# Half of the last weight block stays on chip, and the gathers get six, seven and eleven slots in place of seven, nine and eleven

## The reference

```python
merged = sigmoid(g_nsa) * (o_nsa @ w_br_nsa) + sigmoid(g_dsa) * (o_dsa @ w_br_dsa)
x = x + g1 * (merged @ w_out)
h = rms_norm(x, norm2_g) * (1.0 + sc2) + sh2
q = (h @ peer_wq).reshape(T, 8, 2, 64)                  # the query
s_sub = einsum("thcd,hcnd->thcn", q, subkeys)           # product keys, top 16 -> eidx, gate
for chunk in two chunks of 128 tokens:
    ue, ve = u[ec], v[ec]                               # 128 experts per token, 8 KB each
    act = gelu(einsum("cd,chkd->chk", xc, ue))
    out = einsum("chk,chkd->cd", gc * act, ve)
```

## Time and profile before

| | us |
|---|---|
| median of 3 runs | 981.22 (981.1 to 983.23) |
| profiled execution, its own time | 977.82 |
| profiled execution, span from first to last instruction | 976.0 |
| busy in the span: PE / DVE / ACT / POOL | 800.7 / 645.1 / 409.1 / 283.5 |
| mean granted clock of TensorE | 0.957 of full |

### The profile page before, as it was taken

The page is one execution under the profiler, slowest core; times in us unless marked ns, Lnnn a source line. Parts: engine busy times, 40 slices in busy tenths (PEclk is TensorE's granted clock), DMA queues, the critical chain, the costliest instruction groups (busy, mean ns, idle before and its releaser), DMA issues.

```text
span 976.0 us, 9734 instructions
## 1 busy us (share of the span) xinstructions
PE 800.7 (82%) x2940; PEld 445.9 (46%) x2940; DVE 645.1 (66%) x1663; ACT 409.1 (42%) x1148; POOL 283.5 (29%) x260
## 2 busy tenths in 40 slices
PE   4899969999888989887787788697777778777775
PEld 3644557888873544444454354232322222222221
DVE  4521446996359897886766866867858667586644
ACT  4101132223246887633243634544544344343433
POOL 0000000000033544453343435354253442534420
PEclk8699979998999999999999999999899999999998
DMA  9982403768049999999999999999999999999993
GB/s 373 424 332 92 173 1 111 321 259 344 24 170 424 412 419 419 373 422 418 420 418 419 421 419 420 422 420 422 422 422 421 422 422 421 421 422 422 420 422 125
DMA packets 46899, 342.84 MB, mean 351 GB/s; under 512 B 5312, under 2 KB 6528, under 8 KB 10624
## 3 DMA queue, kind: packets, MB, share of 16 engines
q0 software_dynamic: 36864, 268.45, 66.5%
q1 hardware_dynamic: 9536, 73.31, 18.9%
q10 hardware_dynamic: 448, 0.46, 0.2%
HBM read 341.16 MB, written 1.05 MB: 351 GB/s over the span
## 4 chain that ended last, share of the span: by engine, by line
DMA 45%; PE 27%; DVE 14%; ACT 6%; issue 4%; POOL 2%; SPq 0%; DVEq 0%; POOLq 0%
DMA extra<-in_uv,arena 27%; DMA arena<-in_uv,arena 9%; PE banks L470 7%; DMA ring<-in_uv,arena 7%; PE banks L711 6%; PE banks L504 5%; DVE extra L1480 3%; DMA extra<-in_w_ada 3%; PE banks L664 1%; DVE arena L1480 1%; PE banks L653 1%; PE banks L683 1%; ACT L1002 1%; ACT extra L1012 1%; PE banks L587 1%
## 5 line engine op out<-in xcount | busy, mean ns | idle before, releaser
L711 PE MATMUL banks<-extra 128*128 128x512 f32 x500 | 243.5, 620 | 59.3 <-ACT extra L1012 59.2
L802 POOL DMA_INDIRECT extra<-in_uv,arena x136 | 152.2, 1119 | 459.4 <-DVE arena L1463 315.0
L1002 ACT ACTIVATE arena<-arena 128x1 f32<-128x1 f32 x256 | 51.7, 202 | 323.8 <-DVE arena L1480 323.3
L711 PE MATMUL banks<-arena,extra 128*128 128x512 f32 x296 | 149.1, 633 | 40.0 <-ACT extra L1012 40.0
L711 PEld LDWEIGHTS banks<-extra 128*128 128x128 f32 x500 | 88.7, 193 | 193.5 <-ACT extra L1012 113.9
L1480 DVE CUSTOM_DVE_ANT_0 extra<-extra 128x1024 f32<-128x1024 f32 x80 | 97.9, 1227 | 51.1 <-DMA extra<-in_uv,arena 49.9
L802 POOL DMA_INDIRECT arena<-in_uv,arena x80 | 86.2, 1078 | 129.4 <-PE banks L711 56.4
L711 PEld LDWEIGHTS banks<-arena,extra 128*128 128x128 f32 x296 | 52.9, 196 | 126.9 <-ACT extra L1012 83.7
L1012 ACT ACTIVATE extra<-tab,arena 128x128 f32<-128x128 f32 x235 | 94.3, 401 | 7.7
L1480 DVE CUSTOM_DVE_ANT_0 extra<-extra,arena 128x1024 f32<-128x1024 f32 x56 | 68.6, 1225 | 42.4 <-DMA extra<-in_uv,arena 41.7
L711 PE MATMUL banks<-ring,extra 128*128 128x512 f32 x144 | 73.6, 638 | 26.0 <-ACT extra L1012 26.0
(11 more groups left out here) (242 smaller groups left out, 1064.8 us busy)
## 6 DMA issues: line engine op xcount, KB each, us to landing
arena<-in_w_ada SPq DMA_DIRECT2D x8, 2048.0 KB, 12.1
arena<-in_w_late SPq DMA_DIRECT2D x24, 512.0 KB, 8.3
extra<-in_w_ada SPq DMA_DIRECT2D x4, 2048.0 KB, 10.3
arena<-in_w_in SPq DMA_DIRECT2D x3, 2048.0 KB, 27.4
extra<-in_w_gate SPq DMA_DIRECT2D x3, 2048.0 KB, 8.3
extra<-in_w_br SPq DMA_DIRECT2D x2, 2048.0 KB, 13.9
arena<-in_w_wq SPq DMA_DIRECT2D x2, 2048.0 KB, 18.6
extra<-in_uv,arena POOLq DMA_INDIRECT x136, 18.9
```

Source lines behind the costliest of these rows:

```text
L711: last = nc.tensor.matmul(acc[tt][:, half * 512:(half + 1) * 512], diag[i % DIAGS], uv_slot[SLOT[v]][:, D + half * 512:D + (half + 1) * 51 ...
L802: nc.gpsimd.indirect_dma_start(uv_slot[SLOT[g]], None, A["uv"], bass.IndirectOffsetOnAxis(ap=expert[:, g:g + 1], axis=0)).then_inc(uv_in[S ...
L1002: link(nc.scalar.activation(gel[:, v:v + 1], dots[:, v:v + 1], ACT.Gelu))
```

## The change

Four of the eight query pieces are no longer in the list; the second tile's query takes m 4 to 7 from the 2 MB block that the first tile used, which stays in arena[0:4D] until then. The three late buffers are now arena[4D:5D], arena[5D:6D] and ring[2D:3D]. The gathers have 6 slots up to value 53, 7 up to 123 and 11 from there. The branches of the second tile are done in four pairs, six steps from pair to pair and two within (steps 51, 53, 57, 59, 63, 65, 69, 71, before 51, 53, ... 65), the output projection and all that follows six steps later.

```diff
-LATE = [("br", q, b) for q in range(4) for b in range(2)] + [("out", m, 0) for m in range(KT)] + [("wq", m, 0) for m in range(KT)]
+LATE = [("br", q, b) for q in range(4) for b in range(2)] + [("out", m, 0) for m in range(KT)] + [("wq", m, 0) for m in range(KT // 2)]
 LATE_NO = {c: n for n, c in enumerate(LATE)}
-LSLOTS = 4
+LSLOTS = 3
...
-MORE, MOST = 56, 119
-SLOT = [g % 7 if g < MORE else (7, 8, 0, 1, 2, 3, 4, 5, 6)[(g - MORE) % 9] if g < MOST else
-        (9, 10, 7, 8, 0, 1, 2, 3, 4, 5, 6)[(g - MOST) % 11] for g in range(STEPS)]
+MORE, MOST = 54, 124
+SLOT = [g % 6 if g < MORE else (6, 0, 1, 2, 3, 4, 5)[(g - MORE) % 7] if g < MOST else
+        (7, 8, 9, 10, 6, 0, 1, 2, 3, 4, 5)[(g - MOST) % 11] for g in range(STEPS)]
...
-AT_OT, AT_BR, AT_OUT, AT_SSQ, AT_WQ, AT_H2ROW = 47, 51, 69, 88, 94, 113
-AT_X1ROW, AT_G2ROW, AT_OUT0 = 117, 128, 143
+AT_OT, AT_BR, AT_OUT, AT_SSQ, AT_WQ, AT_H2ROW = 47, 51, 75, 94, 100, 119
+BR_AT = {AT_BR + 6 * (m // 2) + 2 * (m % 2): m for m in range(KT)}
+AT_X1ROW, AT_G2ROW, AT_OUT0 = 123, 134, 149
...
-        uv_slot = [extra[:, 2 * i * D:2 * (i + 1) * D] for i in range(5)] + [arena[:, 2 * i * D:2 * (i + 1) * D] for i in (2, 3)]
-        uv_slot += [ring[:, 2 * i * D:2 * (i + 1) * D] for i in range(2)] + [arena[:, 2 * i * D:2 * (i + 1) * D] for i in range(2)]
-        late = [arena[:, i * D:(i + 1) * D] for i in range(LSLOTS)]
+        uv_slot = [extra[:, 2 * i * D:2 * (i + 1) * D] for i in range(5)] + [arena[:, 6 * D:8 * D]]
+        uv_slot += [ring[:, 2 * i * D:2 * (i + 1) * D] for i in range(2)] + [arena[:, 2 * i * D:2 * (i + 1) * D] for i in range(3)]
+        late = [arena[:, 4 * D:5 * D], arena[:, 5 * D:6 * D], ring[:, 2 * D:3 * D]]
...
-                if tt:
+                if tt and not (kind == "wq" and m >= KT // 2):
                     return piece(pe, kind, m).rearrange("p (k n) -> p k n", k=KT)
...
-                if AT_BR <= g < AT_BR + 2 * KT and (g - AT_BR) % 2 == 0:
-                    branch(1, (g - AT_BR) // 2)
+                if g in BR_AT:
+                    branch(1, BR_AT[g])
...
-                if AT_BR <= g - 2 - BEHIND < AT_BR + 2 * KT and (g - 2 - BEHIND - AT_BR) % 4 == 0:
-                    merge(1, (g - 2 - BEHIND - AT_BR) // 4)
+                if BR_AT.get(g - BEHIND, 0) % 2:
+                    merge(1, BR_AT[g - BEHIND] // 2)
```

## The result

The changed kernel takes 989.5 us (median of 20 runs), the kernel before 981.9 us beside it (20 runs): a ratio of 1.0071, 95% interval 1.0053 to 1.0089. By the ratio it is 7.0 us slower (5.2 to 8.7), where +2.7 was forecast. The ratio is taken over the fast runs; one slow run of each kernel (995.7 and 993.7 us) is in the medians alone.

The account below looks back on a forecast made before the run. The 16 DMA engines were taken as the bound once gathers begin. -5.0 + 2.5 + 2.5 + 2.0 + 0 + 0.7 = +2.7 us, on a median of 981.2, gave 983.9 us; range 978.3 to 988.

Parts of the forecast that it names:

- The bytes, -5.0: DMA-bound stage: four query pieces of 512 KB no longer loaded, 4 x 1.245 us saved, -5.0 us.
- The successor's issue time and the first hole, +2.5: Values 6 to 53: each gather is issued when its successor was; value 13 then lands 2.5 us late.
- The releases do not move: they hang on ACT: First hole: slot releases stay in place, depending on busy ACT and on values landed before the hole.
- The middle, +2.0: Values 27 to 31: later issue and one late piece fewer cost 1.6 to 2.8 us, or 0 if absorbed; +2.0 taken.
- the shallow queue, +0.7: Stretches with few gathers issued ahead grow by some 20 us, costing 0 to 2 us; +0.7 taken.
- The sign that I gave: Before value 54: 6 to 9 us of DMA rate lost in all would show the forecast right.
- The second hole, +2.5: Value 39: issued at 385.35 after VectorE's sum of value 33, it lands 2.5 us late.
- the third rival: Slot 3, holding all VectorE values, sets the pace: eight rounds cost 1.6 us each, +8, 989 us; chance 0.08.
- The filler: Values 27 to 31: three late pieces, four before, have 3.7 us of transfers that fill the hole.
- Values 45 to 53, 0, from -1.3 to +1.3: Waits of perhaps 1.3 us offset by spread landings not losing the same 2.8 us again; 0 taken.
- Values 54 to 123, late buffers, pairs, 0: Seven slots still cover landing, and three late buffers with pairs six steps apart cost nothing: 0.
- the faster one: First rival: gathers into a nearly empty queue land in 6.1 us, giving -2.8, 978.4 us; chance 0.18.

Follow-up runs that it names:

- e1: The kernel before without loading the last four query pieces, the first four read again instead: 0.9935 of the kernel before, -6.4 us.
- e11: The changed kernel with Relu for the second tile's exponential, 22 ACT table loads fewer: 1.0075 of the kernel before, against the changed kernel's 1.0071.
- e12: The kernel before with Relu for the second tile's exponential: 1.0002 of the kernel before.
- e14: The changed kernel with the dot on half the row for values 0 to 53: 1.0003 of the kernel before, 6.7 us faster than the changed kernel.
- e17: The kernel before with the dot on half the row for values 0 to 53: 1.0018 of the kernel before.
- e2: The kernel before with six gather slots in place of seven for values 6 to 55, nothing else: 1.0106 of the kernel before, +10.4 us.
- e4: The changed kernel with every seventh value of the first half summed by VectorE in place of every sixth: 1.0088 of the kernel before.
- e6: The changed kernel with seven slots to value 123, late buffers in the ring, their pieces issued later, branches from step 53: 0.9986 of the kernel before, -1.4 us.
- e3: The changed kernel's timetable and three late buffers in the old memory, seven slots up to 123, all 24 pieces: 0.9985 of the kernel before.
- e13: The changed kernel with PE's value step on half its columns for values 1 to 53: 1.0056 of the kernel before, 1.5 us faster than the changed kernel.

## Why the prediction was wrong, point by point

- **The bytes, -5.0.** Right: -6.4 (4.0 to 8.8) in e1.
- **The successor's issue time and the first hole, +2.5.** Right in the trace: values 12 and 13 are issued when 13 and 14 were, and 13 lands 2.4 us later.
- **"The releases do not move: they hang on ACT".** This is the step that failed. Between value 13 and value 27 the issue times fall another 6.4 us behind those of the successors before, 4.8 of it from value 20 to 23. ACT was not the limit: with its table loads gone neither kernel gains (e11, e12), and after the change it is idle for 3.2 us in the ten where it was idle for 0.7 before. A slot's round is issue, landing, dot, ACT, PE, release. With six slots the round has a median of 17.4 us and six gathers are 14.94, so a late landing can delay the dot, that the release, and that the gather six values on. DVE's part in it is shown: 0.53 us less per dot wins 6.7 us with six slots, about half of what the slot costs, and nothing with seven (e14, e17). The other half is not assigned; PE's value steps at half the clock are in the trace where the largest slip is, and no run tests them.
- **The middle, +2.0, and the shallow queue, +0.7.** Mis-sized for the same reason. I listed holes at values 12, 27 and 39 and let the rate between them be near full. It was 313 to 402 from 320 to 400 us. The whole slot cost +7.7 in my sum, 10.4 alone (e2), 12.3 by the rates of the changed kernel. This 12.3 - 7.7 = 4.6 us is the miss: 7.0 was measured for a forecast of 2.7. The sign that I gave, 6 to 9 us lost in all before value 54, was passed: 15.7 were.
- **The second hole, +2.5, and slot 3.** Value 39 does wait 4.45 us for DVE's sum. But the coincidence with every sixth value, on which I built it and the third rival, makes little or nothing of the loss (e4).
- **The filler.** Taken as three pieces' worth in the middle, and by the traces probably right in kind: e6, without them, loses 4.8 us there. Whether the changed kernel loses more than e2 (12.3 by rates in one trace, 10.4 by runs) is within what traces and intervals leave open; its one piece less (1.2 us) was not tried by itself.
- **Values 45 to 53, 0, from -1.3 to +1.3.** Not borne out: the issue times slip there from 7.2 to 10.1 us behind those of the successors.
- **Values 54 to 123, late buffers, pairs, 0.** Right: 419 GB/s after 432 us, median to landing 13.4 of which 8 suffice, e3 without cost. PE stood for 1.05 us once in front of a branch, at 489.41, and the rate of that stretch stayed full.

The rivals: the landings were not short (only the first gather landed in 6.1 us; 8.3 and 7.2 at the hole), so the faster one is out. The slower one was nearer in size, +8, but by luck: its mechanism is the coincidence that e4 all but rules out.

What stays open: PE's share in the round, its clock with it, and why DVE, which waits for gathers for 25.9 us in this stage, still counts so much. The likely reading is that its time adds to the length of the round, not to its own load; e14 and e17 fit that, but no run separates the two.

## What to carry to other kernels

A buffer ring is a loop. Sum a slot's whole round (issue to landing, use, release, reissue) and set it against slots times the transfer's own time. With five slots, where the transfers are fewest in the queue, the round was 15.4 us (median). 7 x 2.49 = 17.4 us has play for that, 6 x 2.49 = 14.9 has none, and the seventh slot was worth 10.4 us, the sixth another 16.0, in the rate of the whole stage and not in single holes. The round is no constant (17.4 with six slots), so such a sum says about when a loss begins and not how large it is. A release may only be held fixed in a forecast where the row shows its engine at work on something that doesn't descend from the transfer; a busy engine is no proof of that. And before moving small transfers, look whether they fill a pause of the large ones: the saved bytes were worth 6.4 us alone (5.0 by their size) and 1.4 when their neighbours no longer stood in the gap. Last, before an experiment is read as "all of the loss", set it against the right zero: here the version with the same bytes and all slots, 6.4 us below the kernel before.

## What was not expected of the hardware

The busy share of the DMA engines can look full while the rate is 5% down. From 330 to 340 us, after the change, their busy share is 1.00 and the rate 402 GB/s, where before, in the same stretch, a share of 1.01 gave 424. From 380 to 390 the share is 1.01 in both, and the rates are 397 and 418. The stretch before:

```profile
330.00:340.00 10.00, 10.00 (x43) 5.88 (x42) 8.63 (x29) 7.72 (x20) 6.54 (x6) 1.00 1.01 424
```

Half the columns taken from PE's value steps (e13) brought its granted clock from 0.91 to 0.73 of full, that is from mostly 2.4 GHz to about half the time at 1.2. PE's busy time fell by 12.6 us in that stage: the value steps took 21.3 less, all other products 8.7 more.
